# A 22-tile feed-forward loop with split-precision operands: the high and the low activations in one moving operand

## The reference, cut to what matters

```
h = rms_norm(x, g)                       # per token
gate, up = h @ w_gate, h @ w_up          # 1024 -> 2816 each
x = x + 0.5 * (silu(gate) * up) @ w_out  # 2816 -> 1024; blocks 5 and 6: silu(conv(gate)+b), factor 1
```

## Time and profile before

| | |
|---|---|
| median of 3 runs | 2221.65 us (2220.83 to 2225.66) |
| the profiled execution | 2223.43 us |
| its span in the profile | 2221.6 us |
| busy: TensorE matmul / weight load / VectorE / ScalarE | 93 / 90 / 68 / 46 % |
| mean granted TensorE clock | 0.957 of full |
| DMA | 328.06 MB, mean 148 GB/s |
| matmuls | 15894, of which 13392 from three-matmul groups with 256 columns |

### The profile page before, as it was taken

How to read it: one execution, slowest core, us unless ns; L and a number is a source line. 1 busy time by engine, 2 the same in 40 slices (tenths; PEclk the granted TensorE clock), 3 DMA queues, 4 the chain that set the end, 5 groups by cost and what they waited for, 6 DMA issues and landing times.

```text
span 2221.6 us, 40600 instructions
## 1 busy us (share of the span) xinstructions
PE 2065.4 (93%) x15894; PEld 1999.9 (90%) x15894; DVE 1507.2 (68%) x2267; ACT 1032.1 (46%) x1605; POOL 132.0 (6%) x78
## 2 busy tenths in 40 slices
PE   7999999878999999998998799998969999969999
PEld 7999889768999999997987789998969999849999
DVE  6566867557766666677875667656958677676766
ACT  5444543544544544454435344444625454644543
POOL 0000012010000000000310000000600000100000
PEclk9999999989999999999999899998979999969999
DMA  6554532223556555554313244554424554513554
GB/s 223 187 174 153 189 115 76 96 95 105 172 178 181 169 183 176 187 164 142 117 65 105 95 151 153 187 181 157 132 86 159 179 183 157 159 50 114 190 188 133
DMA packets 90964, 328.06 MB, mean 148 GB/s; under 512 B 10224, under 2 KB 11376, under 8 KB 90736
## 3 DMA queue, kind: packets, MB, share of 16 engines
q1 hardware_dynamic: 90288, 324.50, 45.2%
q10 hardware_dynamic: 576, 2.16, 0.3%
HBM read 325.57 MB, written 1.05 MB: 147 GB/s over the span
## 4 chain that ended last, share of the span: by engine, by line
PE 73%; DVE 17%; ACT 4%; DMA 2%; issue 2%; POOL 0%; SPq 0%; ACTq 0%; DVEq 0%
PE ps L1777 72%; DVE w_lo L1008 5%; DMA raw<-stream 2%; ACT w_hi L476 2%; DVE arena L1270 1%; DVE arena L1030 1%; DVE arena L1529 1%; DVE a_lo L1051 1%; PE ps L1952 1%; DVE x L1019 1%; PE ps L2156 1%; POOL sc L924 0%; DVE tmp L1061 0%; DVE arena L1281 0%; DVE arena L1137 0%
## 5 line engine op out<-in xcount | busy, mean ns | idle before, releaser
L1777 PE MATMUL ps<-a_hi,w_hi 128*128 128x256 f32 x4464 | 1283.7, 288 | 36.1 <-DVE a_lo L1051 8.0
L1777 PE MATMUL ps<-a_hi,w_lo 128*128 128x256 f32 x4464 | 1270.4, 285 | 0.0
L1777 PE MATMUL ps<-a_lo,w_hi 128*128 128x256 f32 x4464 | 1262.0, 286 | 0.0
L1777 PEld LDWEIGHTS ps<-a_hi,w_hi 128*128 128x128 f32 x4464 | 868.8, 195 | 45.6 <-issue 19.0
L1008 DVE TENSOR_TENSOR w_lo<-raw,w_hi 128x1024 fp32r<-128x1024 f32 x614 | 753.2, 1233 | 190.7 <-ACT w_hi L476 190.1
L1777 PEld LDWEIGHTS ps<-a_hi,w_lo 128*128 128x128 f32 x4464 | 868.4, 195 | 0.0
L1777 PEld LDWEIGHTS ps<-a_lo,w_hi 128*128 128x128 f32 x4464 | 864.1, 195 | 0.5
L476 ACT ACTIVATE w_hi<-raw 128x1024 fp32r<-128x1024 f32 x614 | 636.2, 1051 | 297.6 <-DMA raw<-stream 169.9
L1071 DVE TENSOR_TENSOR arena<-ps,arena 128x512 f32<-128x512 f32 x132 | 91.1, 690 | 306.2 <-PE ps L1777 306.0
L924 POOL TENSOR_TENSOR sc<-sc,nhalf 128x2 f32<-128x2 f32 (+5 forms) x25 | 60.9, 2440 | 1802.5 <-DVE sc L1035 1317.7
L520 ACT ACTIVATE arena<-arena 128x256 f32<-128x256 f32 x88 | 36.9, 420 | 248.7 <-DVE arena L1071 247.5
(11 more groups left out here) (291 smaller groups left out, 1513.2 us busy)
## 6 DMA issues: line engine op xcount, KB each, us to landing
raw<-stream SPq DMA_DIRECT2D x613, 512.0 KB, 3.7
gates<-late ACTq DMA_DIRECT2D x1, 1088.0 KB, 5.7
out<-x SPq DMA_DIRECT2D x8, 128.0 KB, 2.0
con<-consts SPq DMA_DIRECT2D x1, 800.0 KB, 9.7
raw<-stream ACTq DMA_DIRECT2D x1, 512.0 KB, 3.8
x<-x_in ACTq DMA_DIRECT2D x2, 256.0 KB, 6.2
x<-x_in SPq DMA_DIRECT2D x2, 256.0 KB, 6.0
par<-params SPq DMA_DIRECT2D x1, 451.0 KB, 7.9
```

Of the source, the lines that this page charges most:

```text
L1777: return nc.tensor.matmul(o, a, b, start=start, stop=stop, **k)
```

## The change

The high and the low activations become two halves of one tile `a_both`. `fm_wide` replaces `fm` for gate and up of tiles 1 to 21. It gives TensorE the high and low halves of block k as one moving operand of two runs of 256 columns, 512 in all; left half of the bank: w_hi by a_hi, right half: w_hi by a_lo. The third product is still a matmul of 256 columns, into the left half. So gate takes one bank and up another, and two tiles in flight take banks 4 to 7.

The two halves of each bank must then be added. ScalarE copies the right halves of both banks to SBUF (`low_half`), as the first step of its tile; it waits for the up unit. VectorE waits for that copy and adds the left halves (`added`). The multiplication by the scales (`scaled`) is now an instruction of its own, SBUF to SBUF, placed behind VectorE's first split. TensorE may reuse the banks after `added`. The small norm matmuls move from banks 6 and 7 to bank 5. Tile 0 stays as it was (`scaled_first`).

```
-        a_hi = sb("a_hi", [PART, 20, TOK], F32R)
-        a_lo = sb("a_lo", [PART, 20, TOK], F32R)
+        a_both = sb("a_both", [PART, 2, 20, TOK], F32R)
+        a_hi, a_lo = a_both[:, 0], a_both[:, 1]
...
+            def low_half(p, u_end, j=0):
+                act.wait_ge(unit_used, u_end + 6 * j)
+                nc.scalar.activation(glo, ps[:, 4 + 2 * p:6 + 2 * p, TOK:512], ACT.Copy).then_inc(lo_copied, 1)
...
                     F, p = F0 + f, f % 2
+                    if f:
+                        low_half(p, n0 + (3 * f if f > 1 else 4), j)
                     for u in splits[:1]:
                         split(u + AHEAD, j)
...
+            def added(p, W, j=0):
+                dve.wait_ge(lo_copied, W + 2 * j)
+                V.tensor_tensor(gus[:, p, :].rearrange("p (a b) -> p a b", b=TOK), ps[:, 4 + 2 * p:6 + 2 * p, 0:TOK], glo, ALU.add
+                                ).then_inc(gu_added, 1)
+            def scaled(F, p, j=0):
+                v = gus[:, p, :].rearrange("p (a b) -> p a b", b=TOK)
+                dve.wait_ge(gu_added, wide_tiles(F) + 2 * j)
+                V.tensor_tensor(v, v, each(rrow, 2), ALU.mult).then_inc(gs_ready, 1)
...
-                    scaled(F, p, n0 + (3 * f if f > 1 else 2 * f + 2), j)
+                    if f == 0:
+                        scaled_first(n0 + 2)
+                    else:
+                        added(p, wide_tiles(F), j)
...
-                        for u in splits[:2]:
+                        for u in splits[:1]:
+                            split(u + AHEAD, j)
+                        if f:
+                            scaled(F, p, j)
+                        for u in splits[1:2]:
                             split(u + AHEAD, j)
                         gating(F, p, j)
...
+            def fm_wide(u, b, j=0, middle=None):
+                s = u % SLOTS
+                pe.wait_ge(split_ready, u + 1 + 6 * j)
+                for k in range(KC):
+                    if middle and k == KC // 2:
+                        middle()
+                    w = slice(k * 128, (k + 1) * 128)
+                    mm(bank(b).rearrange("p (a b) -> p a b", b=TOK), w_hi[:, s, w], a_both[:, :, k, :], start=(k == 0), stop=False)
+                    i = mm(bank(b, 0, TOK), w_lo[:, s, w], a_hi[:, k, :], start=False, stop=(k == KC - 1))
+                i.then_inc(unit_used, 1)
...
-                    if F0 + f >= 2:
-                        pe.wait_ge(gs_ready, F0 + f - 1 + 2 * j)
+                    if f > 2:
+                        pe.wait_ge(gu_added, wide_tiles(F0 + f - 2) + 2 * j)
+                    else:
+                        pe.wait_ge(gs_ready, F0 + 1)
                     p = f % 2
-                    fm(u, bank(4 + p, 0, TOK), j)
-                    fm(u + 1, bank(4 + p, TOK, 512), j)
+                    fm_wide(u, 4 + 2 * p, j)
+                    fm_wide(u + 1, 5 + 2 * p, j)
```

More of the change, by code:

```diff
@@ L293, in before, with wide_tiles @@
             return t - sum(n < t for n in FFN_NORMS)
+        def wide_tiles(F):
+            return F - F // FT
         def gate_at(l, i):
@@ L384, in build @@
         ssum = reg(3328, 2, TOK)
+        glo = reg(3840, 2, TOK)
         F2 = 2 * DEPTH * FT
@@ L1031, in square_sums, with variance @@
                                     ).then_inc(sq_sum, 1)
-            def variance(t):
+            def variance(t, b=6):
                 dve.wait_ge(stat_ready, t + 1)
-                V.tensor_scalar(sc[:, 2:4], bank(6, 0, 2), 1.0 / DM, EPS, ALU.mult, ALU.add).then_inc(var_ready, 1)
+                V.tensor_scalar(sc[:, 2:4], bank(b, 0, 2), 1.0 / DM, EPS, ALU.mult, ALU.add).then_inc(var_ready, 1)
             def scales(t):
@@ L1066, in norm, with scaled_first @@
                 low(KC - 1)
-            def scaled(F, p, u_end, j=0):
-                dve.wait_ge(unit_used, u_end + 6 * j)
-                V.tensor_tensor(gus[:, p, :].rearrange("p (a b) -> p a b", b=TOK), bank(4 + p).rearrange("p (a b) -> p a b", b=TOK),
+            def scaled_first(u_end):
+                dve.wait_ge(unit_used, u_end)
+                V.tensor_tensor(gus[:, 0, :].rearrange("p (a b) -> p a b", b=TOK), bank(4).rearrange("p (a b) -> p a b", b=TOK),
                                 each(rrow, 2), ALU.mult).then_inc(gs_ready, 1)
+            def added(p, W, j=0):
[6 more added lines that the diff above has]
+                V.tensor_tensor(v, v, each(rrow, 2), ALU.mult).then_inc(gs_ready, 1)
             def gating(F, p, j=0):
@@ L1111, in ffn @@
                 split(n0 + AHEAD)
-                variance(t)
+                variance(t, 5)
                 split(n0 + 1 + AHEAD)
                 scales(t)
-                V.tensor_copy(rrow, bank(7, 0, TOK)).then_inc(rrow_ready, 1)
+                V.tensor_copy(rrow, bank(5, 0, TOK)).then_inc(rrow_ready, 1)
                 dve.wait_ge(rrow_ready, FFN_NORMS.index(t) + 1)
@@ L1786, in ffn_stat @@
                     for j in range(TT):
-                        i = mm(bank(6, j, j + 1), ssum[:, q, 128 * j:128 * j + 128], ones[:, 0:1], start=(q == 0 and j == 0),
+                        i = mm(bank(5, j, j + 1), ssum[:, q, 128 * j:128 * j + 128], ones[:, 0:1], start=(q == 0 and j == 0),
                                stop=(q == 1), skip_group_check=True)
@@ L1889, in ffn @@
                     fm(n0 + 1, bank(4, TOK, 512))
-                if F0:
-                    pe.wait_ge(gs_ready, F0)
-                fm(n0 + 2, bank(5, 0, TOK), middle=lambda: ffn_stat(t))
-                fm(n0 + 3, bank(5, TOK, 512), middle=lambda: ffn_spread(t))
+                fm_wide(n0 + 2, 6, middle=lambda: ffn_stat(t))
+                fm_wide(n0 + 3, 7, middle=lambda: ffn_spread(t))
                 gate_up(2, n0 + 4)
```

5 lines of the change are left out of this document (2 added, 3 removed).

## The result

The changed kernel takes **2231.14 us** (median of 6 runs, 2229.79 to 2231.59). The kernel before, run beside it, takes 2225.12 us (6 runs, 2220.83 to 2226.61). The ratio is **1.0030** [1.0017, 1.0042]: slower by 6 us where 14 us faster was forecast. The profiled execution took 2229.84 us, 6.4 more than that of before; its mean granted clock is 0.953 of full, against 0.957.

A forecast was written before the change was run, and what follows sets the result against it. TensorE's matmul rate was taken to bound the kernel inside blocks, the uncovered chain at their ends. Terms -25.5 - 0.4 + 9.9 + 2.3 = -13.7 us, from the median 2221.65, gave 2208 us, range 2196 to 2219.

The forecast's parts named there:

- 0.227 + 0.120 = 0.347 against 0.360: Gate and up matmuls: a wide plus a narrow one cost 0.347 us, three narrow ones 0.360; 25.5 us saved over 120 tiles.
- The second run of columns: Wide matmul's moving operand: its second run of 256 columns, 20 KB away, was taken to cost nothing.
- share kept: Rival on the wide matmul: each run of columns pays the fixed share, so nothing is saved; 2233 us, chance 0.10.
- Small part of the share goes, 2228: Rival on TensorE's matmuls: only a fifth of the removed pairs' fixed share is saved, 5.1 us; 2228 us, chance 0.04.
- Costs hidden inside the loop: Inside the tile loop: TensorE covers the added copy and addition, chain 8.35 us within a tile's 8.43; nothing paid.
- The ends, 9.9: At block ends nothing covers the longer chain: 2.1 us later in block 1, 9.9 us given back over six blocks.
- The clock, 2.3: Last down unit: the 2.8 us wait before it lowers the clock at one of five block ends, costing 2.3 us.
- The sum for the blocks: Feed-forward blocks: tiles -25.5, tile 1 -0.4, ends +9.9 and clock +2.3 were to make -13.7 us.
- Tile 1: First wide tile of each block: half its saving goes into waits on the norm's small matmuls; 0.4 us saved in all.
- The rest of the span: Code outside the feed-forward blocks: the prediction gave it no term, so no change in time.

The follow-up runs named there:

- scaling ahead: The changed kernel with VectorE's scaling put directly behind the addition, in front of its first split: 2213.72 us, ratio 0.9962 to the kernel before.
- one run: The changed kernel with high and low activations of each contraction block side by side, so the wide operand is 512 columns in a row: 2227.78 us, ratio 1.0018.
- grouped: The changed kernel with each wide unit's 8 matmuls of 512 columns first, then its 8 of 256, not in turn: 2219.73 us, ratio 0.9988.
- the last one: The changed kernel with grouped matmuls, scaling before the splits, last tile's gating chain first, and two splits behind the update in blocks 1, 3, 4: 2209.98 us, ratio 0.9933.

## Why the prediction was wrong

**The step that failed** is "0.227 + 0.120 = 0.347 against 0.360". Both figures are right for a matmul among its like, and their sum is not the price of the two in turn, which is 0.353. Half of the saving is missing in it: 13.6 us came instead of 25.5. The mean over 144 matmuls in rows 3 hid that the first ones after narrow ones were dearer; the distances at 1896 us would have shown it. With them the sum would have had about 0.232 for a wide matmul, and the forecast would have been near no change (-15.4 - 0.4 + 9.9 + 2.3 = -3.6).

- *The second run of columns*, taken at nothing: **right**, the tile is 8.527 us with one run and with two. The rival "share kept" named 2233 us, close to what was measured, but by a mechanism that isn't there: its tile would be 8.64.
- *Small part of the share goes, 2228*: its picture, that the share grows where one pair is taken out, is nearest to the cause; about half went, not a fifth. The Trainium skill (TensorE: Matmul & The Clock Gate, Back-to-back issue gap) has 2.5 ns for the share, in a formula for an isolated matmul without its weight load, and says nothing of lengths in turn. The traces, with a weight load for each matmul, have 13.3 in pure streams and about 6 on top for each pair in turn; the 2.5 does not hold for them.
- *Costs hidden inside the loop*: **right but for a small part**. A tile is as long as TensorE's matmuls, and no wait on loads (a landing of 3.4 us in the median) or banks appeared. "So nothing is paid inside the loop" missed the one wait for `w_lo` at the start of blocks 5 and 6, 0.7 us together. With the scaling ahead of the split neither block has it.
- *The ends, 9.9*: **right**, 9.2 by the traces. Measured is the time from the start of the chain (the scaling before, the copy after) to the end of the update, in kernels that have the changed kernel's waits and full clock at that end. It grows by 2.1 us in block 1 (changed kernel), 0.6 in block 2 (grouped), 2.1 in block 3 (one run), 1.8 in block 4 (grouped) and 0.6 in block 6; forecast were 2.1, 1.0, 2.1, 2.1 and 0.5. For block 3 that is 965.56 - 953.24 = 12.32 in the one-run kernel against 965.09 - 954.90 = 10.19 before. For block 5 no kernel with this wait has full clock; the changed kernel's 3.4 less 1.4 for the clock stretch leaves 2.0.
- *The clock, 2.3*: the mechanism was right, the number of ends wrong (four, not one), the price of one too high (1.4, not 2.3). Four ends are 5.6 us, and the stretch at the start of block 1 is about 1.2 more (from the first low operand to the last it takes 175.7 us, block 2 takes 174.5): 6.8. The five kernels with a stretch at 26 to 28 us have block 1 longer by 0.7 to 1.5 in this measure, the six others by 0.1 or less.
- *The sum for the blocks*: tiles -13.6, ends +9.2, clock +6.8, waits for `w_lo` +0.7 make +3.1, and +3.1 was measured. That it closes to the tenth is luck: block 5's end and the clock's price are differences of traces, good to a few tenths each. Tile 1, forecast at -0.4, shows no saving.
- *The rest of the span*, which the prediction left at nothing, took 3.3 us more. It isn't a constant: in the eleven kernels the same code (with two splits more behind three updates in the last one) takes 1146 to 1158 us, and the stretches of lower clock in it add up to 185 to 214 us. They go with the time only in part: the longest rest has the most, but with 191 and 192 us it takes 1152 (before) and 1146 (scaling ahead). Nobody can say from these runs which edit moves them where. **This part stays open.**

Against the forecast of -13.7 for the profiled execution stands +6.4, 20.1 us apart: 11.9 from the matmuls' rate, 4.5 from the clock, 3.3 from the rest, 0.7 from the waits for `w_lo`, 0.4 from tile 1, less 0.7 at the ends. The range, 2196 to 2219, fell short since it took the two rates as sure.

## What to carry to other kernels

Take the cost of an instruction from rows where it has the neighbours that it will have: a mean over a long run of its like hides what the first ones cost. Where a step is added to a chain, look for the place where nothing covers it, a loop's last round; there the order of the queue can be worth nearly as much as the saving in the loop (moving one scaling gave the blocks 10.4 us, clock included; all the matmuls removed gave 13.6), and after the wait is gone ask what is queued ahead of the next consumer. And a wait of 2 to 3 us ahead of TensorE's last unit was mostly paid twice here (20 of 28 cases), the second time in clock.

## What the runs showed that was not expected

- Two matmul lengths in turn, 512 and 256 columns, take 0.353 us a pair; in groups of two or of eight 0.348 to 0.349; at their pure rates 0.347.
- After the clock rises within a run of 512-column matmuls the first ones are dearer too: 0.232 us, then 0.226, with no other length near.
- 512 columns in two runs 20 KB apart take as long as in one run: 8.527 us a tile in both.
- Waits of 2.8 to 3.0 us ahead of a block's last down unit were followed, in that unit, by a stretch at half clock in 17 of 25 cases (the changed kernel and the four experiments that kept these waits, five ends each); waits of 1.5 us and less in none; the three waits of 2.0 us, all in block 5, in all three. Which of the long ones it hits is not the same from kernel to kernel with the same wait.
